# A mixture-of-experts gather with its operands exchanged: rows moving, picks stationary, for experts of up to 64 tokens

## What is computed

```python
def moe_ffn(h, router_w, router_b, w1, b1, w2, b2):
    logits = (xt @ router_w + router_b).astype(jnp.float32)
    top_v, top_e = lax.top_k(logits, TOP_K)          # 4 of 32
    gate = jax.nn.softmax(top_v, axis=-1)
    ...
    def expert_block(args):
        rows, e = args
        xb = xt[rows]
        hb = xb @ w1[e] + b1[e]                      # w1[e]: 1024 x 2048
        g, u = hb[:, :D_EXPERT], hb[:, D_EXPERT:]
        g = jnp.minimum(g, SWIGLU_LIMIT)
        u = jnp.clip(u, -SWIGLU_LIMIT, SWIGLU_LIMIT)
        glu = g * jax.nn.sigmoid(g * SWIGLU_ALPHA)
        return ((u + 1.0) * glu) @ w2[e] + b2[e]     # w2[e]: 1024 x 1024
```

## Time and profile before

| | us |
|---|---|
| median of 3 runs | 2575.02 |
| lowest, highest | 2566.83, 2606.62 |
| the profiled execution, timed | 2580.8 |
| its span in the trace | 2579.1 |

### The profile page before, as it was taken

How to read it: one execution, slowest core, us unless ns; L and a number is a source line. 1 busy time by engine, 2 the same in 40 slices (tenths; PEclk the granted TensorE clock), 3 DMA queues, 4 the chain that set the end, 5 groups by cost and what they waited for, 6 DMA issues and landing times.

```text
span 2579.1 us, 32389 instructions
## 1 busy us (share of the span) xinstructions
PE 2275.8 (88%) x12228; PEld 1343.8 (52%) x12229; DVE 589.6 (23%) x1216; ACT 365.2 (14%) x714; POOL 6.5 (0%) x23
## 2 busy tenths in 40 slices
PE   7976797789899898878876999999999999999996
PEld 5655344555564667643334555545455555545553
DVE  3354122212123112530013211212122222212112
ACT  1021101111212002420010111001111111111111
POOL 1000000000000000000000000000000000000000
PEclk9977897799999996678986999989998999989998
DMA  8820242489994533002241999769799999999990
GB/s 292 298 98 0 98 163 98 170 323 333 354 316 174 206 111 124 1 1 98 101 170 39 388 383 382 282 230 349 277 382 381 347 393 373 393 361 392 368 375 17
DMA packets 272763, 621.67 MB, mean 241 GB/s; under 512 B 12200, under 2 KB 19026, under 8 KB 272510
## 3 DMA queue, kind: packets, MB, share of 16 engines
q1 hardware_dynamic: 272302, 616.95, 65.4%
q10 hardware_dynamic: 208, 0.67, 0.1%
HBM read 616.55 MB, written 1.05 MB: 239 GB/s over the span
## 4 chain that ended last, share of the span: by engine, by line
PE 76%; issue 5%; DVE 5%; ACT 2%; ACTq 0%; DVEq 0%
PE pair L1622 25%; PE pair L1415 12%; PE pair L1658 10%; PE pair L1677 8%; PE pair L1695 4%; PE pair L1627 3%; PE pair L1402 3%; PE pair L1661 2%; PE pair L1464 1%; PE pair L1831 1%; PE pair L1456 1%; PE pair L1427 1%; PE pair L1708 1%; PE pair L1439 1%; PE pair L1419 1%
## 5 line engine op out<-in xcount | busy, mean ns | idle before, releaser
L1622 PE MATMUL pair<-ring,r_at 128*64 128x256 f32 (+1 forms) x4864 | 665.3, 403 | 50.4 <-issue 46.6
L1622 PEld LDWEIGHTS pair<-ring,r_at 128*64 128x64 f32 (+1 forms) x4864 | 383.7, 143 | 319.6 <-issue 181.7
L1658 PE MATMUL pair<-ring,r_big 128*64 128x512 f32 x1152 | 265.6, 612 | 0.4 <-issue 0.4
L1415 PE MATMUL pair<-ring,x_T 128*128 128x512 f32 (+1 forms) x608 | 238.8, 548 | 2.4 <-ACT r_big L722 1.0
L1677 PE MATMUL pair<-r_big,r_mix 128*128 128x64 f32 (+1 forms) x1600 | 205.6, 291 | 25.8 <-DVE r_big L1343 15.0
L1677 PEld LDWEIGHTS pair<-r_big,r_mix 128*128 128x128 f32 x1600 | 199.0, 206 | 36.8 <-issue 36.0
L1178 DVE TENSOR_SCALAR r_big<-iota,rank 128x128 f32<-128x128 f32 x100 | 24.1, 284 | 760.2 <-PE pair L1627 583.8
L1415 PEld LDWEIGHTS pair<-ring,x_T 128*128 128x128 f32 x608 | 108.2, 191 | 127.8 <-issue 126.0
L1658 PEld LDWEIGHTS pair<-ring,r_big 128*64 128x64 f32 x1152 | 80.8, 141 | 153.0 <-issue 151.8
L1402 PE MATMUL pair<-x_T,ring 128*128 128x256 f32 x656 | 152.5, 391 | 8.0 <-DVEq L841 6.6
L1402 PEld LDWEIGHTS pair<-x_T,ring 128*128 128x128 f32 x656 | 125.6, 194 | 32.4 <-issue 8.0
(11 more groups left out here) (306 smaller groups left out, 1571.7 us busy)
## 6 DMA issues: line engine op xcount, KB each, us to landing
ring<-exp_w SPq DMA_DIRECT2D x192, 2048.0 KB, 12.3
ring<-w_in SPq DMA_DIRECT2D x24, 2048.0 KB, 9.1
ring<-w_gate SPq DMA_DIRECT2D x16, 2048.0 KB, 10.2
ring<-w_up SPq DMA_DIRECT2D x16, 2048.0 KB, 12.8
ring<-w_down SPq DMA_DIRECT2D x16, 2048.0 KB, 9.2
ring<-mod_w SPq DMA_DIRECT2D x12, 2048.0 KB, 14.1
ring<-w_out SPq DMA_DIRECT2D x4, 2048.0 KB, 9.9
ring<-w_branch SPq DMA_DIRECT2D x3, 2048.0 KB, 7.6
```

Of the source, the lines that this page charges most:

```text
L1415: ins = mm(out[:, t, 0:n], xT[:, k, P * t:P * t + P], w[:, k, c0:c0 + n], start=(k == 0), stop=(k == nk - 1 and bias is None))
L1622: ins = mm(out, stat(k), w_[:, k, c0:c0 + n], start=(k == 0), stop=(bias is None and k == KD - 1))
L1658: ins = mm(ps[2][H2 * h:H2 * h + H2, 0:512], hT[:, at:at + H2], cols, start=beg, stop=end)
```

## The change

In stage 2 the call of `gather` is split in two. For the next expert with up to 64 tokens, `pick_rows` makes four products with `pick` stationary (64 columns) and 512 columns of `HT` moving, two side by side; the result is the gathered rows, 64 places by 512 features in each half of the partitions, in the first bank of `ps[1]`. ScalarE copies it to SBUF (`XR`, an unused part of `r_u`) and signals `rows_read`; `turn_rows` then makes four 128x128 transposes into the second bank, and ScalarE's `rows_of` copies those into `XG`. For the next expert with more tokens, `pick_rows` only signals, and `turn_rows` does the gather of before, now behind the second `turn_hidden`. Stage 1 is unchanged.

```diff
@@ (buffers)
+        XR = r_u[:, 1024:1536]
@@ rows_of
+                    if b == 2 and w == H2:
+                        s.copy(XG[:, :, 0:n].rearrange("p (h c) s -> p c h s", h=2),
+                               ps[1][:, 512:1024].rearrange("p (c h s) -> p c h s", c=4, h=2))\
+                            .then_inc(sem("xg_ready2"), 1)
+                        return
@@ ScalarE
-            act.wait_ge(sem("gathered2"), 1)
+            def rows_read(e):
+
+                def body(w):
+                    if w == H2:
+                        act.wait_ge(sem("rows_picked"), e + 1)
+                        s.copy(XR, ps[1][:, 0:512]).then_inc(sem("rows_read"), 1)
+                    else:
+                        act.sem_inc(sem("rows_read"), 1)
+
+                return body
...
                     turned(2, 0, e, w)
+                    by_size(act, size_next, rows_read(e + 1))
+                    turned(2, 1, e, w)
                     by_size(act, size_next, rows_of(2, e + 1))
-                    turned(2, 1, e, w)
@@ TensorE
+            def pick_rows(e, buf, size):
+
+                pe.wait_ge(sem("picked2"), e + 1)
+
+                def body(w):
+                    if w != H2:
+                        pe.drain().then_inc(sem("rows_picked"), 1)
+                        return
+                    for t in range(NT):
+                        for h in range(2):
+                            ins = mm(ps[1][H2 * h:H2 * h + H2, 0:512], pick[:, buf, t, 0:H2],
+                                     HT[:, t, 512 * h:512 * h + 512], start=(t == 0), stop=(t == NT - 1))
+                    ins.then_inc(sem("rows_picked"), 1)
+
+                by_size(pe, size, body)
+
+            def turn_rows(e, buf, size):
+
+                pe.wait_ge(sem("rows_read"), e + 1)
+
+                def body(w):
+                    if w == T:
+                        pe.drain().then_inc(sem("gathered2"), 1)
+                        return
+                    if w == H2:
+                        for c in range(4):
+                            ins = nc.tensor.transpose(ps[1][:, 512 + P * c:512 + P * c + P], XR[:, P * c:P * c + P],
+                                                      ident)
+                    else:
+                        for k in range(KD):
+                            for t in range(NT):
+                                ins = mm(ps[1][:, P * k:P * k + w], HT[:, t, P * k:P * k + P], pick[:, buf, t],
+                                         start=(t == 0), stop=(t == NT - 1))
+                    ins.then_inc(sem("gathered2"), 1)
+
+                by_size(pe, size, body)
@@ expert, b == 2
                         pe.wait_ge(up_free, 2 * e + 2)
-                        gather(b, e + 1, 1 - buf, size_next)
+                        pick_rows(e + 1, 1 - buf, size_next)
                         pe.wait_ge(hidden, 2 * e + 2)
                         pe.wait_ge(hiddenT, 2 * e + 1)
                         turn_hidden(b, 1, size)
+                        turn_rows(e + 1, 1 - buf, size_next)
```

More of the change, by code:

```diff
@@ L804, in _ @@
                                   accum_out=rt_s[:, 224 + t:225 + t]), "route2_exped")
-            act.wait_ge(sem("gathered2"), 1)
+            def rows_read(e):
[6 more added lines that the diff above has]
+                return body
+            act.wait_ge(sem("rows_picked"), 1)
+            by_size(act, size_of(act, 0), rows_read(0))
             by_size(act, size_of(act, 0), rows_of(2, 0))
@@ L1766, in expert @@
                     turn_picks(b, buf, size)
-                gather(b, 0, 0, size_of(pe, 0))
+                if b == 1:
+                    gather(b, 0, 0, size_of(pe, 0))
+                else:
+                    pick_rows(0, 0, size_of(pe, 0))
+                    turn_rows(0, 0, size_of(pe, 0))
                 with looped(pe, 0, n // PASS) as i:
```

## The result

| | before | after |
|---|---|---|
| median of 20 runs each, us | 2578.2 | 2605.3 |
| lowest, highest | 2566.8, 2606.6 | 2599.4, 2614.1 |
| span of the profiled execution | 2579.1 | 2612.3 |
| second expert stage in it (first up-product to last product) | 1157.5 | 1178.4 |

A forecast was written before the change was run, and what follows sets the result against it. TensorE was taken to set the pace, transfers 1% behind. The terms, capped by the weights, gave 32 us; less 4 for returning clock falls, 28 us: 2553 for this execution, 2547 against the median 2575.0 (-1.1%), range 2532 to 2571.

The forecast's parts named there:

- What bounds the kernel: Second expert stage: TensorE sets the pace, weight transfers 1% behind, 32.7 us against 33.0 us per expert.
- Term 1: Gather of a small expert: eight products replace 32 instructions, so down-products start 0.58 us earlier, in 28 transitions.
- the 1.9 among the signs: Sign to look for in the trace: ScalarE's new copy 1.9 us behind VectorE's L1343.
- Term 2: In front of four large experts: the gather now stands behind the second transposes, 1.0 us lost each.
- Term 3: Clock falls to 1.2 GHz at the gather, in five small experts and one large, go away: 23.5 us gained.
- the sign by which the prediction called itself wrong altogether: The clock falls having another cause than the gather, with two thirds of the gain hanging on them.
- Term 4: Weight transfers at 385 GB/s allow at most 26 of 30 us from 1867.2 to 2500.6 us; 32 us in all.
- Rival (b): Stalls at the loop's jump grow and eat 24 us of the gain: 2567 to 2575, say 2572 us; chance 0.12.
- (a): Clock falls stay, since the new wait and transposes are thin work too: 12 us gained, 2563 us; chance 0.23.
- (c): The two 64-column products don't run side by side: 38 us slower, 2613 us; chance 0.05, with other round-trip mishaps.
- (d): The transfers allow more, with shorter stalls behind the jumps: 45 us gained, 2530 us; chance 0.10.

The follow-up runs named there:

- a_short: The changed kernel without TensorE's second-stage bodies for experts of over 128 tokens, which never run here: 2542.4 us, 0.984 of the kernel before.
- b_short: The kernel before without TensorE's second-stage bodies for experts of over 128 tokens, which never run here: 2544.5 us, 0.987 of the kernel before.
- b_light: The kernel before with each stage-2 weight load bringing a quarter of its rows, the rest stale: 2538.7 us, 0.983 of the kernel before.
- a_late_short: The changed kernel without the never-run bodies for over 128 tokens, and with `turn_rows` behind the first half of the down-products: 2530.3 us, 0.980 of the kernel before.
- a_nowait: The changed kernel without the wait for ScalarE's copy, its transposes reading token rows already there: 2580.2 us, 0.998 of the kernel before.

## Why the prediction was wrong

**What bounds the kernel** failed, and the rest with it. "TensorE sets the pace, and the transfers are 1% behind it" left out a third supplier, the code. Removing only code that never runs gained 1.3%, and moving the loop by 64 instructions lost 2.3%, with TensorE's instructions unchanged. TensorE's 7 us of idle time per pass, 5 of them behind the jump, and the falls of the clock were the visible part.

**Term 1** was right in its parts. Eight instructions take 1.94 us with the array's emptying (1.73 + 0.17 said), the copy starts 2.15 us behind the end of VectorE's limit (2.1 by the sum; the 1.9 among the signs does not follow from it), TensorE waits 0.42 us (0.65 said). With code at hand the expert gets 0.54 us shorter (a_short; 0.58 said). In after, 0.58 us of waiting for instructions ahead of the down-products take it back.

**Term 2** was too small. The second transposes start 1.71 us behind the first, as worked out, but between them and the gather lie 0.5 to 0.8 us of "issue", and the gather takes 3.8 us. The down-products start 6.5 to 8.1 us behind the first transposes instead of 5.6, the longest two where the gather ran partly at 1.2 GHz. The same four took 5.0, 5.2, 5.2 and 5.2 us before, not the 4.63 that the term set against them. That is 1.7 + 1.3 + 2.8 + 2.9 = 8.7 us lost instead of 4.

**Term 3** had the place right and the cause wrong. The falls in the gathers of small experts are gone in the changed kernel, and TensorE's busy time fell by 41 us. But the low level moved more than it went: it holds for 81 us of the stage before and for 71 after, now mostly around the loop's jump, as in this window:

```profile
2158.20:2168.40 10.20, 5.66 (x28) 3.38 (x30) 0.00 (x0) 0.00 (x0) 0.00 (x0) 0.50 0.80 317
```

And b_short kept the old gather and had 24 us of it in its stage, b_light 10. So the gather alone does not make the clock fall; that was the sign by which the prediction called itself wrong altogether. What the falls need besides is open; in b_short and b_light they went together with a part of the idle time that has no releaser (28.0 us ahead of up-products before, 19.5 and 6.8 there). In before the packets came at their own rate while TensorE ran slowly, and a faster TensorE waits for the same packets; that is argued, since no run made the falls alone go. Two thirds of the forecast gain hung on this term.

**Term 4** took 385 GB/s for the full rate. With fewer packets of code the weights moved at 392, and 388 in the shifted kernel, so the weights were not the cap that it worked out; in after no wait for weights appears at all. They were the limit only in a_short and a_late_short.

**Rival (b)** had the mechanism: "the stalls at the loop's jump grow". It was priced so that it could at most eat the gain (2572), and it was limited to the jump. The jump's idle time grew by 3 us in a pass (8.2 against 5.2), and 11 us more stand ahead of down-products. With the bound failed a sentence beside this rival: that the shorter code "moves the places where code pages end; I give that no sign". That put at nothing a term of up to 62 us from the best to the worst place, more than every term of the sum; it should have been a case of its own with both signs. At the best place of its four the changed kernel measured 0.8% faster than before, so that the sign of the result was in part luck of the place. Rivals (a), (c) and (d) did not occur: the falls left the gathers of small experts, and 0.24 us per instruction say that the two 64-column products run side by side.

## What to carry to other kernels

Where a loop has many bodies chosen at run time, look at the instruction queue's packets in a pass before reading idle time as anything else. Their number times their mean interval is always the length of the pass and proves nothing; take the interval where they stand closest together in long runs (5.9 us here). If the number times that one is near the pass (21 x 5.9 = 124 of 132 us), test it by taking out bodies that never run: here that gave 1.3%. Shorten the code there first; and judge a small change to such a kernel only over several placements of its loop, since one placement can be worth more than the change. A wait added on the engine that is short of code can cost more than its idle time (17 to 25 us for 12.5 here, at one place of the loop).

## What was not expected of the hardware

- One packet of 16 KB came every 5.8 to 6.3 us beside weights at 383 GB/s, and every 6 to 13 us in b_short, where fewer were wanted; beside a quarter of the weights the shortest intervals were 3.1 to 4.0 us.
- A likely reason why the wait for the copy cost up to twice its idle time, which was only argued: while the engine's sequencer stands in a wait it does not reach the next packet, so that packet is asked for later. In after, intervals of 7.8 to 8.2 us stand among those of 5.8 to 6.0; in a_nowait, with the same code at the same places, the longest in such a pass is 7.4.
- The loop has some 20 packets, and all of them are fetched again in each pass: 21, 21 and 21 in the three passes of before ahead of the last. Of a pass's 5150 instructions TensorE executes 914 products and 914 weight loads, and some 200 others.
- Taking out code that never ran brought back TensorE's clock in a gather that was left as it was: 81 us at 1.2 GHz in the stage before, 24 in b_short.
